# Second-layer gates and banded queries: eight-matmul units, or pairs of tiles in seven block products

## The reference

```python
pl = split_cols(h @ w_in, ODD_SPLITS)        # latent tokens
pc = split_cols(hc @ w_in, ODD_SPLITS)       # context tokens
...
ya = head_rmsnorm(oa_lat, ml_norm_g) * silu(pl[3])       # gates 0 to 3
q = axial_rope(heads(pl[5], SW_HEADS), rows, cols)       # banded queries, 4 tiles of 128
yb = merge(swa_attn(q, k, v, kc, vc, sink)) * silu(pl[8])  # gates 4 to 7
```

## Time and profile before

| | |
|---|---|
| median of 3 runs | 1600.25 us (1599.61 to 1601.06) |
| profiled execution, span | 1600.2 us |
| TensorE matmuls busy | 1515.5 us, 95% |
| VectorE, ScalarE, GpSimd busy | 757.7, 570.1, 35.8 us |
| chain that ended last, on TensorE | 76% |
| HBM traffic | 86 GB/s over the span |
| second layer's scans, about | 1030 to 1238 us |
| second layer's attention, about | 1238 to 1473 us |

### The profile page before, as it was taken

One profiled execution on the slowest core, in us unless ns is written; L12 is line 12 of the kernel. 1 busy time (PEld: TensorE's weight loads), 2 busy tenths in 40 slices (PEclk: granted clock), 3 DMA queues, 4 the chain that ended last, 5 costly groups with the idle time before them and its releaser, 6 DMA issues.

```text
span 1600.2 us, 25568 instructions
## 1 busy us (share of the span) xinstructions
PE 1515.5 (95%) x9656; PEld 1039.9 (65%) x9656; DVE 757.7 (47%) x1653; ACT 570.1 (36%) x1320; POOL 35.8 (2%) x108
## 2 busy tenths in 40 slices
PE   7999989999899899898999999999999999999996
...
GB/s 379 96 27 14 14 104 22 81 157 28 167 83 60 148 70 78 183 14 15 118 120 159 200 66 54 76 72 63 56 80 25 107 14 14 15 27 35 171 158 125
DMA packets 72037, 139.80 MB, mean 87 GB/s; under 512 B 6656, under 2 KB 44588, under 8 KB 70572
## 3 DMA queue, kind: packets, MB, share of 16 engines
...
...
## 4 chain that ended last, share of the span: by engine, by line
PE 76%; DVE 9%; issue 9%; ACT 4%; DMA 1%; SPq 0%; POOL 0%; DVEq 0%; ACTq 0%; POOLq 0%
PE proj L1250 16%; PE mixed L1250 14%; PE mixed L1234 4%; PE proj L1237 4%; PE turned L1358 4%; PE mixed L1200 4%; PE turned L1340 4%; PE proj L1234 3%; PE scores L1200 2%; ACT vstage L2095 2%; PE scores L1318 2%; PE mixed L1237 2%; PE scores L1321 2%; ACT work L2095 1%; PE scores L1250 1%
## 5 line engine op out<-in xcount | busy, mean ns | idle before, releaser
L1250 PE MATMUL proj<-hT,weights 128*128 128x512 f32 (+1 forms) x752 | 314.3, 564 | 3.0 <-ACT vstage L2095 2.1
L1250 PE MATMUL mixed<-hT,weights 128*128 128x512 f32 (+1 forms) x672 | 259.1, 534 | 1.5 <-DMA weights<-in_weights 0.9
L1250 PEld LDWEIGHTS proj<-hT,weights 128*128 128x128 f32 x752 | 138.3, 192 | 132.0 <-issue 128.2
L1250 PEld LDWEIGHTS mixed<-hT,weights 128*128 128x128 f32 x672 | 125.4, 194 | 100.6 <-issue 93.8
L2095 ACT ACTIVATE work<-turned 128x512 f32<-128x512 f32 (+2 forms) x136 | 72.7, 534 | 145.9 <-PE turned L1340 106.9
L1794 DVE TENSOR_TENSOR yT<-turned,work 128x128 f32<-128x128 f32 x72 | 21.0, 291 | 159.3 <-PE turned L1358 135.0
L2095 ACT ACTIVATE work<-work,stat 128x640 f32<-128x640 f32 (+8 forms) x98 | 74.0, 755 | 31.8 <-DVE stat L1765 29.8
L1340 PE MATMUL turned<-consts,work 128*128 128x128 f32 (+3 forms) x448 | 69.1, 282 | 10.9 <-DVE yT L1794 8.6
L1340 PEld LDWEIGHTS turned<-consts,work 128*128 128x128 f32 (+3 forms) x448 | 48.6, 139 | 42.9 <-issue 19.1
L1234 PE MATMUL mixed<-weights,hT 128*128 128x256 f32 x320 | 71.1, 379 | 0.0
L1234 PEld LDWEIGHTS mixed<-weights,hT 128*128 128x128 f32 x320 | 60.2, 190 | 9.0 <-issue 1.2
...
## 6 DMA issues: line engine op xcount, KB each, us to landing
...
work<-rows SPq DMA_DIRECT2D x32, 128.0 KB, 3.4
```

What stands on the lines that cost most here:

```text
L1250: last = nc.tensor.matmul(PJ[BANK_OF[u]][:, 0:n], weights[:, w % WBUFS, k, :], src[:, k, t0:t0 + n], start=(k == 0), stop=(k == KT - 1))
```

## The change

Two weight tiles become a pair, and each pair's 256 output features by 1024 latent tokens are computed as a two-by-two block product with seven block products in place of eight. A tile's features split in two halves of four (`a11`, `a12` and `a21`, `a22`), the tokens too, and a product is four matmuls of 512 columns over one half of the depth. Context tokens are untouched: gates and queries use latent tokens alone.

- Sums of weight halves (four a pair, 512 columns each) are made on GpSimd, partly in place in the weight buffers (`s_tile_sum`).
- Sums of token halves are made once on VectorE: three for each of four depth tiles during the first half of the scans (`s_token_parts`), and one of 4 x 512 in place in `hT`, when the last other reader of it is done (`s_token_last`).
- The products run in the order 1, 6, 2, 7, 5, 4, 3. Product 2 is added in PSUM onto product 1, which ScalarE has copied out as `upper`; VectorE adds 6 to it, then 7 into `lower`, and finishes the quarters 5, 4 and 3 from them. Two banks are held across the products, and `make_schedule` keeps account of which are in use.
- Gates 0 to 3 are kept out of `yT` until their quarter is complete (`kept_apart`); the gate's multiplies stand one product later (`quarter_gated`).
- The query quarters of products 5, 4 and 3 are added and rotated on VectorE with no ScalarE copy; the scale goes into the rotation.
- The order: value projection `vv` moves from the third part of the scans to the first; the second part is the keys alone; pairs (gates 4, 5), (gates 6, 7) and (queries 0, 1) fill the third; pairs (gates 0, 1), (queries 2, 3) and (gates 2, 3) fill the attention, of which the last head pair has no filler.
- Some buffers move: a part of `consts`, the widened sums, the second query tile's rotated rows, one raw output tile that is loaded later.

The diff, cut to its core (`s_pair` issues on TensorE, `rotate` on VectorE, `s_tile_sum` on GpSimd):

```diff
+TILE_PAIRS = ((("gate", 1, 4), ("gate", 1, 5)), (("gate", 1, 6), ("gate", 1, 7)), (("sw", 0, "q"), ("sw", 1, "q")),
+              (("gate", 1, 0), ("gate", 1, 1)), (("sw", 2, "q"), ("sw", 3, "q")), (("gate", 1, 2), ("gate", 1, 3)))
+PRODUCTS = (1, 6, 2, 7, 5, 4, 3)
+QUARTER_OF = {2: (0, 0), 5: (1, 1), 4: (1, 0), 3: (0, 1)}
...
+def pair_products(g, following=None):
+    x1, x2, y1, y2, y3 = (Slot() for _ in range(5))
+    slot = {1: x1, 2: x1, 6: y1, 7: y2, 5: x2, 4: y2 if kept_apart(g) else y3, 3: x2}
...
+    for m in PRODUCTS:
+        steps = [("pair", g, m, part, slot[m], stage.get(m)) for part in range(2)]
+        late = {7: 2, 4: 5, 3: 4}.get(m)
+        gated = [("quarter_gated", g, late, stage[late])] if late and gate else []
+        out += steps[:1] + gated + steps[1:]
+        if m == 7:
+            out.append(("tile_sum", g, 3))
+        if following is not None and m in (5, 4):
+            out += [("tile_sum", following, x) for x in ((0, 1) if m == 5 else (2,))]
+    return out + ([("quarter_gated", g, 3, stage[3])] if gate else [])
...
-    first = k[:4] + g[8] + k[4:8] + g[9] + k[8:] + v
...
-    s += scans(1, [first, project(("sw", 0, "k"), "kk", CHUNKS_ALL) + g[12], third])
-    last = attention(1, [rq[1] + g[0], rq[2] + g[2], rq[3] + g[4], g[5] + g[7]], [g[1], g[3], g[6]])
+    first = k[:4] + v[:8] + k[4:8] + vv[:4] + k[8:] + v[8:] + vv[4:]
+    for x in range(4):
+        first.insert(12 + 8 * x, ("token_parts", 1, x))
+    second = kk + [("tile_sum", 0, x) for x in range(3)]
+    pairs = [pair_products(g, g + 1 if g + 1 < len(TILE_PAIRS) else None) for g in range(len(TILE_PAIRS))]
+    s += scans(1, [first, second[:-3], second[-3:] + [("token_last", 1)] + pairs[0] + pairs[1] + pairs[2]])
+    (one, two), (three, four) = cut_after(pairs[3], 11), cut_after(pairs[5], 3)
+    four, five = cut_after(four, 7)
+    last = attention(1, [one, pairs[4], four, []], [two, three, five])
...
+            def s_pair(g, m, part, u, stage):
+                left = {1: one[:, 0:4], 6: sum_two, 2: one[:, 4:8], 7: two[:, 0:4], 5: sum_one, 4: two[:, 4:8], 3: one[:, 4:8]}[m]
...
+                    if m == 6:
+                        pe.wait_ge(*at(("token_parts", 1, 3)))
+                        pe.wait_ge(*at(("tile_sum", g, 2)))
+                    if m == 2:
+                        pe.wait_ge(*at(("first_copied", g)))
...
+                    last = nc.tensor.matmul(to, left[:, k, :], right, start=begins, stop=(k == 3), skip_group_check=True)
...
+            def rotate(kind, t0, n, st, stage, scale):
+                link(V.stream_shuffle(dst, st, [(r + 16) % 32 for r in range(32)]))
+                link(V.scalar_tensor_tensor(out=dst, in0=dst, scalar=scale, in1=tables[:, LAT + lo:LAT + lo + n],
+                                            op0=ALU.mult, op1=ALU.mult))
+                link(V.scalar_tensor_tensor(out=st, in0=st, scalar=scale, in1=tables[:, lo:lo + n],
+                                            op0=ALU.mult, op1=ALU.mult))
+                link(V.tensor_tensor(dst, dst, st, ALU.add), ("stage_used", stage), ("rotated", *kind, t0),
+                     *([("filled", "sw", kind[1], "rq")] if (t0 + n == T) != bool(kind[1] % 2) else []))
...
+            def s_tile_sum(g, x):
+                    linked(pool.tensor_tensor(sum_one, a21, a22, ALU.add), ("tile_sum", g, 0))
...
+                    linked(pool.tensor_tensor(a21, a11, a21, ALU.subtract), ("tile_sum", g, 1))
...
+                        pool.wait_ge(*at(("pair", g - 1, 6)))
+                    linked(pool.tensor_tensor(sum_two, sum_one, a11, ALU.subtract), ("tile_sum", g, 2))
...
+                    linked(pool.tensor_tensor(a12, a12, sum_two, ALU.subtract), ("tile_sum", g, 3))
```

249 lines of the change are left out of this document (226 added, 23 removed).

## The result

| | before | after |
|---|---|---|
| median of the runs on one chip | 1599.61 us | 1607.3 us |
| range | 1595.6 to 1601.06 | 1601.52 to 1608.82 |
| profiled execution, span | 1600.2 us | 1606.5 us |
| first scores of the second layer's attention at | 1237.85 | 1250.17 |
| first product of the output projection behind it at | 1473.53 | 1479.82 |

The ratio is 1.0046, with a 95% interval of 1.0026 to 1.0066: the change makes the kernel slower by 0.26 to 0.66%, some 7.4 us, where 12.9 us faster was forecast. (One disturbed run of the changed kernel, 4342.26 us, is left out of the ratio and the range but not of its median, which is 1606.0 without it.)

A forecast was written before the change was run, and what follows sets the result against it. The prediction took TensorE, its matmuls filling 95% of the span, as the bound. Its terms, -20.9 + 1.2 - 1.8 + 4.0 + 1.5 + 4.0 - 3.4 + 2.5 = -12.9, gave 1587.3 us, range 1579 to 1598.

The forecast's parts named there:

- The 24 matmuls: Second layer's gate and query units: 168 matmuls instead of 192, at 0.87 us each, -20.9 us if nothing new waits.
- the term with the widest ends: Attention steps without filler: 4.75 us instead of 6.11, so less gained than credited, +4.0 us (0 to 17.4).
- the rival that named the chain: Attention: unfilled steps stay at 6.11 us because their chain takes 5.95; 1600.7 us, no change; chance 0.12.
- The rival that gave 1607.3: Last head pair: TensorE drops to 1.2 GHz in half of ten steps with gaps, +20 us; chance 0.08.
- rows 10 and 11: Profile rows: TensorE's granted clock at 0.50 after waits of 3.15 and 1.85 us; used for the handover's +1.5 us.
- the value products ... keep their price: Scans: value products moved from the third part to the first cost the same there; 0 us.
- other bank and row waits in the scans: Scan steps: products or turns wait for banks that VectorE frees behind its scan chain; +1.2 us (0 to 3).
- handover to the first scores: Scans to attention: first scores wait for an uncovered rotation of five VectorE operations, +4.0 us, plus +1.5 for slow clock.
- two gate ends: Attention: two waits remain at gate pairs' ends, 1.7 us each, 3.4 in place of 6.8; -3.4 us.
- rotations of queries (2, 3): Attention: three rotations of five VectorE operations in a row bring waits of about 1 us each; +2.5 us net.
- 0, both ends: Weight sums on GpSimd, 1.4 us each: hidden behind TensorE's products, so they cost 0 us.
- the whole gain: Rival: unfilled steps lose 2, rotations nothing, handover waits 2 and keeps the clock; -20.9 us, 1579.3 us; chance 0.17.

The follow-up runs named there:

- e3: The changed kernel with the last gate multiply of the two gate pairs in the attention placed behind the next step's product and minima on VectorE; ratio 1.0014.
- P1: The kernel before, with idle VectorE additions put into five attention steps just ahead of its product with the gate sums; one run, 1623.8 us.
- e1: The changed kernel with every weight sum on GpSimd cut from 512 columns to 8, that part of the computation left out; ratio 1.0044.
- E14: e12 with every weight sum on GpSimd cut to 8 columns, that part of the computation left out; ratio 0.9933.
- e10: The changed kernel with later gate multiplies, queries (0, 1) before gates (6, 7), two more multiplies held back, and value chunks whole between scan steps; ratio 0.9949.
- e12: e10 with the key units of the scans' second part aligned to its three steps; ratio 0.9979.
- e13: e12 with the second query pair begun earlier in the attention and its last two rotations placed behind the next step's minima on VectorE; ratio 0.9965.

## Why the prediction was wrong

**Right.** The 24 matmuls are gone and the others keep their pace: eight of the profile's begin at 1205.62 and what follows them at 1209.06, 3.44/4 = 0.86 each. The sums on GpSimd take 1.26 to 1.71 us (forecast 1.4), and TensorE waits for none. A step without filler was put at 4.75, the term with the widest ends. It is 4.72, as TensorE's transposes in three of them show:

```profile
1453.68 0.44 PE L1474 MATMUL turned<-consts,pair 128*128 128x128 f32 x2 [0.30 <-ACT work L2321]
1458.41 0.44 PE L1474 MATMUL turned<-consts,work 128*128 128x128 f32 x2 [0.30 <-ACT work L2321]
1463.13 0.44 PE L1474 MATMUL turned<-consts,work 128*128 128x128 f32 x2 [0.30 <-ACT work L2321]
```

So the rival that named the chain is out. The rival that gave 1607.3 came out at the measured number by luck: it saw the slow clock in half of ten thin steps of the last head pair, +20, and in this profile these steps run at 1.00 and 4.72. The five falls stood behind single long waits at other places, as the forecast's own rows 10 and 11 had shown. Its mechanism is not excluded: in e3 and six other runs one fall, 1.2 to 1.7 us, did stand in the last of these steps, behind a wait of 1.42.

**Wrong, term by term**, forecast against the profile, in us:

| term | forecast | profile | its clock |
|---|---|---|---|
| "the value products ... keep their price" | 0 | 3.98 | 1.4 |
| other bank and row waits in the scans | +1.2 | +2.4 | |
| handover to the first scores | +4.0, clock +1.5 | 6.25 | 2.0 |
| two gate ends, "1.7 each" | 2 x 1.7 | 3.07 and 3.47 | 1.4 and 2.7 |
| rotations of queries (2, 3) | +2.5 | 1.05 + 2.16 + 0.75 | 3.0 |

- *The clock* is the dearest miss: one fall was counted, 1.5, five came, 10.5. The forecast had the rows for it, a fall behind 3.15 and behind 1.85 us, and used them at one place alone. P1 shows that it comes behind waits in a kernel with all its work, too. The changed kernel's other runs have a mean clock of 0.981 to 0.987, so the 10.5 is that of one execution.
- *"Two remain ... 1.7 each."* The 6.8/7 averages four waits of 1.39 at gates with three of 0.43. Of the former kind, on ScalarE and then VectorE:

```profile
1305.80 0.60 ACT L2095 ACTIVATE vstage<-proj 128x512 f32<-128x512 f32 x1
...
1306.53 0.69 DVE L1642 TENSOR_TENSOR yT<-yT,proj 128x512 f32<-128x512 f32 x1 [2.41 <-ACT vstage L2095]
1307.92 0.69 DVE L1644 TENSOR_TENSOR yT<-yT,vstage 128x512 f32<-128x512 f32 x1 [0.70 <-ACT vstage L2095]
```

  The end of gates (0, 1) has two things more. ScalarE begins 2.05 us after TensorE has left the gate's product (1315.04 to 1317.09), where it began after 1.11 (1304.69 to 1305.80), since VectorE first does two multiplies of the quarter before and the addition of this one. And both of VectorE's multiplies, not one, come behind ScalarE's last operation, 0.7 more. 1.39 + 0.94 + 0.7 = 3.03, beside the 3.07 that TensorE waits; the forecast had added one multiply to the average. E3 took these waits out, for 5 us.
- *"0, both ends"* for GpSimd looked for who waits for the sums. It did not ask whom they hold up: 7 us of VectorE's time, 2.0 of them in the handover, where 6.25 stood for the forecast 4.0; e1, without the hold, has 4.24 there, so the forecast's five operations were priced well. E14 shows a cost that e1 could not.
- *The values* "keep their price" as work, but not in their new place: a chunk that a scan step cuts takes its bank twice.

Forecast and result lie 20 us apart (12.9 and 7.4). Exchanging places alone brought back 15.5 of it (e10). What e10 still lacks of the whole gain, 20.9 - 8.2 = 12.7, is about what its 28.1 us of waits, 9.4 more than before has, and its two falls, 3.1, come to. How much of that a better order would free stays open: e12 and e13 only moved it.

The range was also too narrow by the forecast's own terms. The bounds that it names, added straight, reach from 1576.8 to 1601.0; it gives 1581 to 1596 and does not say how. The result lies outside either.
